# First modulation of layer 0 taken in two halves of rows, with the first weight slot of the projection between them

## The chip, the cores and the metric

The kernel runs on one core of a Trainium2 chip. The metric is the device time in microseconds (us) of one execution; the median of the runs is given. Engines: PE is TensorE (PEld its weight loads), DVE is VectorE, ACT is ScalarE, SP is SyncE, which here only issues transfers.

## The reference, cut to what matters

Two transformer blocks in a row on 256 tokens of width 1024; the change touches only the start of layer 0 of the first block:

```python
c_act = jax.nn.silu(c)                              # (1, 1024)
mod = c_act @ ada_w[layer] + ada_b[layer]           # 6 x 1024 columns
sh1, sc1, g1, sh2, sc2, g2 = split(mod, 6)
h = _rms_norm(x, norm_mix[layer]) * (1.0 + sc1) + sh1
proj = h @ w_in[layer]                              # 1952 columns, first of the mixer
```

So the first projection needs the shift `sh1` (columns 0 to 1023 of `ada_w`) and the scale `sc1` (columns 1024 to 2047). Feature k of `h`, and with it row k of `w_in`, needs only element k of each.

## The kernel before, in words

All weights come as one stream of slots in the order of `plan()`, each at most 128 x 2048 floats (1 MB), into a ring of four slots (`RING`). SP issues the loads in that order (`Sync.load_to`, L398); before load m it waits until the last user of load m - 4 is done (`last_use`). A projection weight is split by ACT into a high part (`whi`, L384) and by DVE into the rest (`wlo`, L338), half a slot at a time (a "chunk"), and PE multiplies each block of 128 rows three times (high by high, low by high, high by low, `mm3`, L240) for two halves of the tokens.

The start (functions `pe_start`, `act_start`, `dve_start`). The 2048 modulation columns are made in four units u of 512 columns; each unit takes two slots, rows 0 to 511 and rows 512 to 1023. For a unit,

- `pe_mods` (PE) multiplies the first slot by the vector `cact` into one row of PSUM: eight passes of 512 columns, since there are four blocks of rows at two passes each;
- `dve_mods` (DVE) multiplies and sums the second slot into `modsum` (tile name `gate`) with four instructions, then copies PE's row to `modrow`;
- `pe_mods_turn` (PE) turns both into a column, with 16 matmuls of one column;
- `dve_mods_turn` (DVE) adds the bias and stores four columns of `K.mod`.

Unit 0 and 1 are the shift, 2 and 3 the scale. `pe_mods(u)` waits until `modrow` of u - 1 has left its bank; `pe_mods_turn(u)` waits for `modrow` of u and until `mods` of u - 1 has left the other bank. In between PE transposes x (`pe_turn`, line L249) and spreads the row norms (`pe_along`, to `cbm` by ACT). Then `dve_mod_scale` makes the scale (`sc`), and `dve_mod_t` (DVE) and `act_mod_t` (ACT) make the eight blocks of `h` transposed: DVE multiplies into `aux`, ACT adds the shift (`hT`), DVE makes the rest (`hTl`). The splits of the weight chunks are placed between the blocks by `split_between`: chunk 1 behind block 2, chunk 2 behind block 4, chunk 3 behind block 6. `pe_rows` for key `inA0` (416 columns, two slots, four chunks of two blocks) then multiplies, block k waiting for `hT` and `hTl` of k (`ready`). Behind it come `inD0` and the other projections, whose splits and sums run in an order fixed on each engine.

The SP order at the start is: columns, loads 0 and 1, a constant, loads 2 and 3, x, loads 4 to 10, the other constants (1 MB), loads 11 and on. Loads 0 to 7 are the modulation, 8 and 9 `inA0`, 10 the first slot of `inD0`.

Of the kernel before, what the change touches and what calls it, by code (L numbers as in the profile page):

```python
# [76 lines left out]
def ada(layer, c0, c1):  # L77
    return panels(f"ada{layer}", "ada_w", (layer,), KT, c0, c1)
# [5 lines left out]


def plan():
    p = ada(0, 0, 2048)
    for l in range(2):
        into = [panels(f"inA{l}", "w_in", (l,), KT, 768, 1184), panels(f"inD{l}", "w_in", (l,), KT, 0, 512),
                panels(f"qup{l}", "w_q_up", (l,), 2, 0, 768) + panels(f"kvup{l}", "w_kv_up", (l,), 1, 0, 1024),  # L90
                panels(f"inB{l}", "w_in", (l,), KT, 1184, 1696),
                narrow(f"inV{l}", "w_in", (l,), 512, 768) + narrow(f"inV{l}", "w_in", (l,), 1696, 1952)]
        mod = summed(0, 2048) if l == 0 else []
        behind = {(1, 0), (1, 1), (2, 3), (3, 0)}
        for n, stage in enumerate(into):
            for at, slot in enumerate(stage):
                p.append(slot)
                if mod and (n, at) in behind:
                    p.append(mod.pop(0))
        if l == 0:  # L100
            p += summed(0, 3072) + summed(0, 4096)
        p += tapered(f"out{l}", "w_out", (l,))
        if l == 0:
            ffn = gate_up("ffn", "ffn_w_gate", "ffn_w_up", (0,)) + down("ffnd", "ffn_w_down", (0,))
            mod = summed(0, 5120) + [slot for c in range(0, 6144, 1024) for slot in summed(1, c)]
            for n, slot in enumerate(ffn):
                p += [slot] + (mod[n - 2:n - 1] if n > 1 else [])
        else:
            for e in range(NE):
                p += gate_up(f"moe{e}", "moe_w_gate", "moe_w_up", (0, e))  # L110
                p += down(f"moe{e}d", "moe_w_down", (0, e))
    w = "w_in_2"
    xbc = blocks_t("xbc", w, (0,), list(range(XBC0, XBC0 + 4096, 128)))
    p += xbc[:5] + panels("dt", w, (0,), KT, DT0, DT0 + 32) + xbc[5:]
    for c in (Q0, K0, V0):
        p += narrow("qkv0", w, (0,), c, c + 512)
    p += panels("z", w, (0,), KT, Z0, Z0 + 2048)
    p += panels("gs", w, (0,), KT, GS0, GS0 + 1024)
    p += panels("sproj", "w_ssd_proj_2", (0,), 16, 0, D)
    for g in (1, 2):  # L120
        for c in (Q0, K0, V0):
            p += narrow(f"qkv{g}", w, (0,), c + 512 * g, c + 512 * g + 512)
    p += narrow("ga", w, (0,), GA0, GA0 + 1024)
    p += panels("aproj", "w_attn_proj_2", (0,), 4, 0, D)
    p += tapered("out2", "w_out_2", (0,))
    p += blocks_t("up2", "w_up_2", (0,), [c for b in range(FT) for c in (128 * b, FF + 128 * b)])
    p += down("down2", "w_down_2", (0,))
    return p
# [400 lines left out]
def pe_start(K, pe):  # L529

    pe_mods(K, pe, 0)
    pe_mods(K, pe, 1)
    pe_mods_turn(K, pe, 0)
    pe_mods(K, pe, 2)
    pe_mods_turn(K, pe, 1)
    pe_turn(K, pe, "nm0", lambda j, i: K.x[:, i, 128 * j:128 * j + 128], KT, "v")
    pe_mods(K, pe, 3)
    pe_mods_turn(K, pe, 2)
    pe_along(K, pe, "nm0")
    pe_mods_turn(K, pe, 3)  # L540


# [14 lines left out]
def dve_start(K, v):  # L557
    v.wait_ge(K.s_cols, 32)
    v.wait_ge(K.act, "rout_hi")
    v.tt(K.rout[:, 1, :], K.col("router", 0, 64), K.rout[:, 0, :].bitcast(F32), ALU.subtract, key="rout_lo")  # L560
    ang, n, r = K.ang, K.angn, K.angr
    v.copy(K.posf[:, :], K.posi[:, :])
    for i in range(2):
        v.ts(ang[:, i, :], K.col("invf", 0, 16), K.posf[:, i:i + 1], None, ALU.mult)
    for t, (shift, quarter) in enumerate(((0.0, 0.0), (0.25, float(np.float32(np.pi / 2))))):
        v.ts(n[:, :, :], ang[:, :, :], float(np.float32(1 / (2 * np.pi))), shift, ALU.mult, ALU.add)
        v.ts(n[:, :, :], n[:, :, :], MAGIC, None, ALU.add)
        v.ts(n[:, :, :], n[:, :, :], MAGIC, None, ALU.subtract)
        if t:
            v.wait_ge(K.act, ("turn", 0))  # L570
        v.stt(r[:, :, :], n[:, :, :], -TWO_PI_1, ang[:, :, :], ALU.mult, ALU.add)
        v.stt(r[:, :, :], n[:, :, :], -TWO_PI_2, r[:, :, :], ALU.mult, ALU.add)
        v.stt(r[:, :, :], n[:, :, :], -TWO_PI_3, r[:, :, :], ALU.mult, ALU.add)
        v.ts(r[:, :, :], r[:, :, :], quarter, 3.1415925, ALU.add, ALU.min)
        v.ts(r[:, :, :], r[:, :, :], -3.1415925, None, ALU.max, key=("angle", t))
    K.dve.here("angles")
    dve_mods(K, v, 0)
    dve_mods(K, v, 1)
    dve_mods_turn(K, v, 0)
    dve_eps(K, v, "nm0")  # L580
    dve_root(K, v, "nm0")
    dve_mods(K, v, 2)
    dve_mods_turn(K, v, 1)
    dve_mods(K, v, 3)
    dve_mods_turn(K, v, 2)
    v.split_to(1)
    dve_mods_turn(K, v, 3)


def act_squares(K, a, s, p, c0, c1, after):  # L590
# [22 lines left out]
def dve_eps(K, v, s):  # L613
    v.wait_ge(K.act, (s, "sq", 0, 1))
    v.ts(K.ssq[:, 0:2], K.ssq[:, 0:2], EPS, None, ALU.add, key=(s, "eps"))
# [120 lines left out]
            a.act(K.hT[:, j, :], K.rtmp4[:, j % 4, :], ACT.Identity, bias=shift[:, j:j + 1], key=(s, "hi", j), own=False)  # L736


def dve_mod_scale(K, v, layer, which, gain):
    v.stt(K.sc[:, :], K.mod[:, layer, 8 * which + 8:8 * which + 16], 1.0, K.col(gain, 0, 8), ALU.add, ALU.mult)  # L740
    v.last()


# [1 line left out]
    return K.mod[:, layer, 8 * which:8 * which + 8]  # L745


def dve_mod_t(K, v, s, scale, shift=None):

    def low(j):  # L750
        v.wait_ge(K.act, (s, "hi", j))
        src, hi = K.rtmp4[:, j % 4, :], K.hT[:, j, :].bitcast(F32)
        if shift is None:
            v.tt(K.hTl[:, j, :], src, hi, ALU.subtract, key=(s, "lo", j), own=False)
        else:
            v.stt(K.hTl[:, j, :], src, shift[:, j:j + 1], hi, ALU.add, ALU.subtract, key=(s, "lo", j), own=False)
    v.wait_ge(K.act, (s, "along"))
    for j in range(KT):
        v.wait_ge(K.pe, (s, "t", j // 2 * 2))
        if j >= 4:  # L760
            v.wait_ge(K.dve, (s, "lo", j - 4))
        v.stt(K.rtmp4[:, j % 4, :], turned(K, j, TURNED.get(s, (4, 5, 6, 7))), scale[:, j:j + 1], K.along, ALU.mult, ALU.mult,
              key=(s, "v", j), own=False)
        if j:
            low(j - 1)
        split_between(K, v, s, j)
    low(KT - 1)


def pe_rows(K, pe, key, lhs, kt, banks=(0, 1, 2, 3), by=(("dve", 0), ("dve", 1)), block=None, at_part=None):  # L770
# [85 lines left out]
def pe_mods(K, pe, u):  # L856

    pe.wait_ge(K.act, "cact")
    pe.take(ROW)
    m = K.mods[2 * u]
    pe.wait_ge(K.full[m % RING], 16 * (m // RING + 1))
    for k in range(4):
        pe.mm(K.ps[ROW][0:1, :], K.cact[:, k:k + 1], K.ring[:, m % RING, 512 * k:512 * k + 512], k == 0, k == 3,
              done=("mod", u) if k == 3 else None)
    pe.given(ROW, (K.dve, ("modrow", u)))
# [28 lines left out]


def dve_mods_turn(K, v, u):
    v.wait_ge(K.pe, ("modturn", u))  # L900
    v.tt(K.mod[:, 0, 4 * u:4 * u + 4], K.ps[COLUMN][:, 0:4], K.col("ab0", 4 * u, 4), ALU.add, key=("mods", u))


def pe_broadcast(K, pe, s, banks):
# [322 lines left out]
def pe_mixer(K, pe, l):  # L1227
# [9 lines left out]

    def values(x):
        pe_values(K, pe, s, x, js[x])
    pe_rows(K, pe, f"inA{l}", hrows(K), KT, by=COPIES, block=ready(K, pe, f"nm{l}"))  # L1240
    pe_rows(K, pe, f"inD{l}", hrows(K), KT, by=COPIES, banks=BANKS_D)
    pe.wait_ge(K.s_rest, 32)
    pe.wait_ge(K.dve, (s, "low", "rows"))
# [1447 lines left out]
def vector_program(K, v):  # L2691
    dve_start(K, v)
    for l in range(2):
        if l:
            dve_root(K, v, f"nm{l}")
        else:
            dve_mod_scale(K, v, 0, 0, "nm0")
        dve_mod_t(K, v, f"nm{l}", K.sc, shift_of(K, l, 0))
        if l:
            barrier(K, v, ("ffn", 0))  # L2700
        else:
            v.wait_ge(K.s_rest, 32)
        dve_mixer(K, v, l)
        dve_root(K, v, f"nf{l}")
        dve_mod_t(K, v, f"nf{l}", K.sc, shift_of(K, l, 3))
        barrier(K, v, ("mixed", l))
        if l == 0:
            dve_dense(K, v)
        else:
            dve_moe(K, v)  # L2710
    dve_eps(K, v, "n1")
    v.split_to(K.parts["xbc"][0] + 1)
    dve_root(K, v, "n1")
    v.split_to(K.parts["xbc"][0] + 2)
    dve_mod_t(K, v, "n1", K.col("n1", 0, 8))
    barrier(K, v, ("ffn", 1))
    dve_ssd(K, v)
    barrier(K, v, "ssd")
    dve_gated(K, v)
    barrier(K, v, "gated")  # L2720
    dve_windows(K, v)
    dve_merge(K, v)
    dve_root(K, v, "n2")
    dve_mod_t(K, v, "n2", K.col("n2", 0, 8))
    barrier(K, v, "second")
    dve_second_ffn(K, v)
    K.dve.here("end")
# [327 lines left out]
```

## Time and profile before

| | us |
|---|---|
| median of 3 runs | 2193.22 |
| the three runs | 2196.7, 2193.22, 2183.3 |
| the profiled execution | 2187.65 |
| span of its trace | 2185.9 |
| PE busy (share of the span) | 2008.5 (92%) |
| DVE busy | 1670.3 (76%) |
| ACT busy | 1329.2 (61%) |

The span runs from the first to the last instruction of the core; the 1.75 us beside it are outside. The stage that the change touches ends 57.9 us after the span's start. The rest of the kernel is the same in both. The clock granted to PE has two levels, 2.4 GHz (shown as 1.00) and 1.2 GHz (0.50).

### The profile page before, as it was taken

The page shows a single profiled execution, that of the slowest core. Times are in us where ns is not written, and L with a number is a line of the kernel's source. Part 1 is how long each engine was busy: PE and PEld are TensorE (multiplying, and loading weights), DVE is VectorE, ACT ScalarE, POOL GpSimd, SP SyncE. Part 2 cuts the span into 40 slices and gives each one's busy share as a digit, 9 for nine tenths or more (in the row PEclk, how much of TensorE's full clock was granted, in tenths as well). Part 3 has the DMA queues.
Part 4 walks back from the last instruction along what each step waited for, and adds up shares of the span by engine and source line. Part 5 has one row for each costly group of instructions (what it writes and reads, how often), then busy time and mean ns, then how long its engine had stood idle before and what let it go on. Part 6 is the DMA issues. An engine that isn't in the chain of part 4 may idle for free. (4 is left out here: it accounts for less than half of the span.)

```text
span 2185.9 us, 28021 instructions
## 1 busy us (share of the span) xinstructions
PE 2008.5 (92%) x11093; PEld 1729.2 (79%) x11093; DVE 1670.3 (76%) x2154; ACT 1329.2 (61%) x1968; POOL 0.2 (0%) x4
## 2 busy tenths in 40 slices
PE   7868999987799999999999999979999988889999
PEld 4668778876788888888888887769877878878987
DVE  5876888676669989998998999768655655567873
ACT  2645443366568777787877777656556544536652
POOL 0000000000000000000000000000000000000000
PEclk8977999998889999999999999989999989889999
DMA  7634788731239989998998998645314532224543
GB/s 292 225 109 151 259 317 329 261 140 39 97 151 368 360 330 366 366 360 325 361 364 341 357 368 316 248 179 181 136 48 154 195 114 97 97 96 143 186 162 108
DMA packets 70090, 497.20 MB, mean 227 GB/s; under 512 B 8000, under 2 KB 8256, under 8 KB 10688
## 3 DMA queue, kind: packets, MB, share of 16 engines
q1 hardware_dynamic: 69664, 494.28, 61.4%
q8 instruction: 90, 1.47, 0.3%
q10 hardware_dynamic: 288, 1.05, 0.1%
q14 instruction: 48, 0.39, 0.0%
HBM read 494.25 MB, written 1.05 MB: 227 GB/s over the span
## 5 line engine op out<-in xcount | busy, mean ns | idle before, releaser
L338 DVE TENSOR_TENSOR wlo<-ring,whi 128x1024 fp32r<-128x1024 f32 (+1 forms) x845 | 1016.6, 1216 | 288.4 <-ACT whi L384 267.4
L384 ACT ACTIVATE whi<-ring 128x1024 fp32r<-128x1024 f32 (+1 forms) x845 | 886.3, 1054 | 517.8 <-PE ps L236 449.8
L236 PE MATMUL ps<-whi,hT 128*128 128x256 f32 (+2 forms) x944 | 324.5, 344 | 26.7 <-DVE hTl L292 6.4
L236 PE MATMUL ps<-wlo,hT 128*128 128x256 f32 (+2 forms) x944 | 318.7, 338 | 0.0
L236 PE MATMUL ps<-whi,hTl 128*128 128x256 f32 (+2 forms) x944 | 318.1, 337 | 0.0
L236 PE MATMUL ps<-whi,xg 128*128 128x512 f32 (+1 forms) x768 | 290.4, 378 | 5.4 <-DVE wlo L338 5.2
L236 PE MATMUL ps<-whi,xgl 128*128 128x512 f32 (+1 forms) x768 | 286.5, 373 | 0.0
L236 PE MATMUL ps<-wlo,xg 128*128 128x512 f32 (+1 forms) x768 | 286.4, 373 | 0.0
L236 PEld LDWEIGHTS ps<-whi,hT 128*128 128x128 f32 x944 | 186.7, 198 | 50.6 <-issue 6.8
L236 PE MATMUL ps<-whi,hf 128*128 128x512 f32 x528 | 209.4, 397 | 11.0 <-DVE wlo L338 4.7
L236 PE MATMUL ps<-wlo,hf 128*128 128x512 f32 x528 | 207.0, 392 | 0.0
L236 PEld LDWEIGHTS ps<-wlo,hT 128*128 128x128 f32 x944 | 186.8, 198 | 16.7
L236 PEld LDWEIGHTS ps<-whi,hTl 128*128 128x128 f32 x944 | 186.0, 197 | 17.5
L236 PE MATMUL ps<-hT,whi 128*128 128x256 f32 (+1 forms) x616 | 176.2, 286 | 5.9 <-DVE hTl L285 4.0
L236 PE MATMUL ps<-hT,wlo 128*128 128x256 f32 (+1 forms) x616 | 175.8, 285 | 0.0
L236 PE MATMUL ps<-hTl,whi 128*128 128x256 f32 (+1 forms) x616 | 174.9, 284 | 0.0
L236 PEld LDWEIGHTS ps<-whi,xg 128*128 128x128 f32 x768 | 145.3, 189 | 31.2 <-DVE wlo L338 6.3
L236 PEld LDWEIGHTS ps<-whi,xgl 128*128 128x128 f32 x768 | 145.2, 189 | 25.7
L236 PEld LDWEIGHTS ps<-wlo,xg 128*128 128x128 f32 x768 | 145.4, 189 | 24.6
L236 PE MATMUL ps<-whi,hf1l 128*128 128x512 f32 x352 | 137.4, 390 | 0.0
L236 PEld LDWEIGHTS ps<-whi,hf 128*128 128x128 f32 x528 | 99.8, 189 | 32.3 <-DVE wlo L338 5.5
L236 PEld LDWEIGHTS ps<-hT,whi 128*128 128x128 f32 (+1 forms) x616 | 117.4, 191 | 6.9 <-ACT hT L364 4.5
(283 smaller groups left out, 2645.1 us busy)
## 6 DMA issues: line engine op xcount, KB each, us to landing
ring<-in_wstream SPq DMA_DIRECT2D x462, 1024.0 KB, 5.0
ring<-in_wstream SPq DMA_DIRECT2D x4, 832.0 KB, 6.0
ring<-in_wstream SPq DMA_DIRECT2D x6, 256.0 KB, 2.7
cst<-in_cst SPq DMA_DIRECT2D x1, 1028.0 KB, 7.7
x<-in_x SPq DMA_DIRECT2D x1, 1024.0 KB, 13.9
work<-in_bias ACTq DMA_DIRECT2D x2, 512.0 KB, 5.0
ring<-in_wstream SPq DMA_DIRECT2D x2, 512.0 KB, 3.8
out_x<-x SPq DMA_DIRECT2D x1, 1024.0 KB, 4.1
```

The costliest lines, as they stand in the source:

```text
L236: i = self.e.matmul(out, lhsT, rhs, start=start, stop=stop, skip_group_check=True)
L338: i = self.e.tensor_tensor(K.wlo[:, q % NS, 0:cols], src, hi.bitcast(F32), ALU.subtract)
L384: i = self.e.activation(K.whi[:, q % NS, 0:cols], K.ring[:, m % RING, at:at + cols], ACT.Copy)
```

## The change

The plan puts units of the first half of the features first: unit 0 (shift, columns 0 to 511) and unit 1 (now the scale's columns 1024 to 1535). Then comes the first slot of `inA0`, then unit 2 (shift 512 to 1023) and unit 3 (scale 1536 to 2047), then the second slot of `inA0`. So loads 0 to 3 are units 0 and 1, load 4 is the first slot of `inA0`, loads 5 to 8 are units 2 and 3, load 9 the second slot; from 10 on all is as before.

PE does units 0 and 1, both turns, the transposes, `pe_along`, `pe_mods(2)`, and then chunks 0 and 1 of `inA0` (blocks 0 to 3). At chunk 2 it does `pe_second_half`: turn 2, `pe_mods(3)`, turn 3. DVE makes scale and blocks 0 to 3, then the sums of units 2 and 3, then scale and blocks 4 to 7. ACT's program is not edited.

```diff
 def plan():
-    p = ada(0, 0, 2048)
+    p = ada(0, 0, 512) + ada(0, 1024, 1536)
...
                 p.append(slot)
+                if (l, n, at) == (0, 0, 0):
+                    p += ada(0, 512, 1024) + ada(0, 1536, 2048)
...
     pe_mods(K, pe, 1)
     pe_mods_turn(K, pe, 0)
-    pe_mods(K, pe, 2)
     pe_mods_turn(K, pe, 1)
     pe_turn(K, pe, "nm0", lambda j, i: K.x[:, i, 128 * j:128 * j + 128], KT, "v")
+    pe_along(K, pe, "nm0")
+    pe_mods(K, pe, 2)
+
+
+def pe_second_half(K, pe):
+
+    pe_mods_turn(K, pe, 2)
     pe_mods(K, pe, 3)
-    pe_mods_turn(K, pe, 2)
-    pe_along(K, pe, "nm0")
     pe_mods_turn(K, pe, 3)
...
     dve_eps(K, v, "nm0")
+    dve_mods_turn(K, v, 1)
     dve_root(K, v, "nm0")
+    v.split_to(1)
+    dve_mod_scale(K, v, 0, 0, "nm0", 0, 4)
+    dve_mod_t(K, v, "nm0", K.sc, shift_of(K, 0, 0), 0, 4)
     dve_mods(K, v, 2)
-    dve_mods_turn(K, v, 1)
     dve_mods(K, v, 3)
     dve_mods_turn(K, v, 2)
-    v.split_to(1)
     dve_mods_turn(K, v, 3)
+    dve_mod_scale(K, v, 0, 0, "nm0", 4, 8)
+    dve_mod_t(K, v, "nm0", K.sc, shift_of(K, 0, 0), 4, 8)
...
-def dve_mod_t(K, v, s, scale, shift=None):
+def dve_mod_t(K, v, s, scale, shift=None, j0=0, j1=KT):
...
-    for j in range(KT):
+    for j in range(j0, j1):
...
-        if j:
+        if j > j0:
             low(j - 1)
...
 def dve_mods_turn(K, v, u):
+    at = (0, 8, 4, 12)[u]
...
-    pe_rows(K, pe, f"inA{l}", hrows(K), KT, by=COPIES, block=ready(K, pe, f"nm{l}"))
+    pe_rows(K, pe, f"inA{l}", hrows(K), KT, by=COPIES, block=ready(K, pe, f"nm{l}"),
+            at_part=None if l else lambda n: pe_second_half(K, pe) if n == 2 else None)
```

## Rows read from the trace of the kernel before

**Rows 1.** The page: its first line, then part 1 (busy time, share, instructions).

```profile
span 2185.9 us, 28021 instructions
...
PE 2008.5 (92%) x11093; PEld 1729.2 (79%) x11093; DVE 1670.3 (76%) x2154; ACT 1329.2 (61%) x1968; POOL 0.2 (0%) x4
```

**Rows 2.** Timeline: start, duration, engine, operation, count [idle before, releaser]; units and turns.

```profile
8.85 6.03 PE L236 MATMUL ps<-ring,cact 128*1 128x512 f32 x8 [8.85 <-DMA ring<-in_wstream]
...
15.65 3.59 PE L236 MATMUL ps<-ring,cact 128*1 128x512 f32 x8 [0.77 <-DVE modrow L306]
...
19.18 0.38 PE L236 MATMUL ps<-cst,modrow 1*128 1x1 f32 x2
...
21.76 0.16 DVE L285 TENSOR_TENSOR mod<-ps,cols 128x4 f32<-128x4 f32 x1 [1.74 <-PE ps L236]
...
22.71 5.29 PE L236 MATMUL ps<-ring,cact 128*1 128x512 f32 x8 [0.98 <-DMA ring<-in_wstream]
...
25.06 0.48 DVE L277 TENSOR_SCALAR gate<-ring,cact 128x512 f32<-128x512 f32 x1 [0.40 <-DMA ring<-in_wstream]
25.59 2.32 DVE L292 SCALAR_TENSOR_TENSOR gate<-ring,cact,gate 128x512 f32<-128x512 f32 x3
...
28.03 0.68 DVE L306 COPY modrow<-ps 1x512 f32<-1x512 f32 x1
...
30.34 3.19 PE L249 MATMUL ps<-cst,x 128*128 128x128 f32 x16
...
33.46 3.98 PE L236 MATMUL ps<-ring,cact 128*1 128x512 f32 x8
...
39.78 0.69 PE L236 MATMUL ps<-cst,rs 128*128 128x128 f32 x4
...
41.02 0.55 PE L236 MATMUL ps<-cst,modrow 1*128 1x1 f32 x2
...
42.02 0.58 PE L236 MATMUL ps<-cst,modrow 1*128 1x1 f32 x2
...
44.18 0.16 DVE L285 TENSOR_TENSOR mod<-ps,cols 128x4 f32<-128x4 f32 x1 [1.45 <-PE ps L236]
```

**Rows 3.** Timeline, same columns: from the weight split to the end of the first projection.

```profile
40.79 1.67 ACT L384 ACTIVATE whi<-ring 128x832 fp32r<-128x832 f32 x2
...
44.38 0.17 DVE L292 SCALAR_TENSOR_TENSOR sc<-mod,cols 128x8 f32<-128x8 f32 x1
...
46.28 0.69 PE L236 MATMUL ps<-whi,hT 128*128 128x416 f32 x1 [2.13 <-DVE hTl L292]
...
46.83 1.02 DVE L338 TENSOR_TENSOR wlo<-ring,whi 128x832 fp32r<-128x832 f32 x1
...
48.28 0.51 ACT L366 ACTIVATE hT<-aux,mod 128x256 fp32r<-128x256 f32 x1 [1.21 <-DVE aux L292]
...
55.50 2.36 DVE L338 TENSOR_TENSOR wlo<-ring,whi 128x1024 fp32r<-128x1024 f32 x2 [0.62 <-ACT whi L384]
...
57.87 0.52 ACT L364 ACTIVATE work<-ps 128x416 f32<-128x416 f32 x1 [1.53 <-PE ps L236]
```

**Rows 4.** Windows: stretch, length; busy PE, PEld, DVE, ACT, POOL; PEclk, DMA share, GB/s.

```profile
24.00:26.00 2.00, 2.00 (x4) 0.33 (x3) 1.46 (x6) 0.00 (x0) 0.00 (x0) 0.51 1.01 426
...
34.00:36.00 2.00, 2.00 (x6) 0.35 (x5) 0.00 (x0) 0.00 (x0) 0.00 (x0) 0.93 0.07 25
...
42.00:44.00 2.00, 2.00 (x9) 1.94 (x9) 0.73 (x1) 0.46 (x1) 0.00 (x0) 0.50 1.03 428
```

**Rows 5.** Windows of line L236 alone: stretch, length, PE, PEld, PEclk, DMA share, GB/s.

```profile
46.28:51.27 4.99, 4.99 (x15) 4.76 (x16) 0.50 0.89 327
51.27:57.87 6.60, 6.60 (x36) 6.58 (x35) 1.00 0.59 214
```

**Rows 6.** DMA issues in 48 to 52 us, and landing times of L413 in 0 to 80 us.

```profile
ring<-in_wstream SPq DMA_DIRECT2D x1, 1024.0 KB, 4.8
...
DMA to landing us min/median/max: 2.7/7.7/12.8
```

More of the change, by code:

```diff
@@ L736, in act_mod_t, with dve_mod_scale @@
             a.act(K.hT[:, j, :], K.rtmp4[:, j % 4, :], ACT.Identity, bias=shift[:, j:j + 1], key=(s, "hi", j), own=False)
-def dve_mod_scale(K, v, layer, which, gain):
-    v.stt(K.sc[:, :], K.mod[:, layer, 8 * which + 8:8 * which + 16], 1.0, K.col(gain, 0, 8), ALU.add, ALU.mult)
+def dve_mod_scale(K, v, layer, which, gain, j0=0, j1=KT):
+    at = 8 * which + 8
+    v.stt(K.sc[:, j0:j1], K.mod[:, layer, at + j0:at + j1], 1.0, K.col(gain, j0, j1 - j0), ALU.add, ALU.mult)
     v.last()
@@ L763, in dve_mod_t @@
               key=(s, "v", j), own=False)
-        if j:
+        if j > j0:
             low(j - 1)
         split_between(K, v, s, j)
-    low(KT - 1)
+    low(j1 - 1)
 def pe_rows(K, pe, key, lhs, kt, banks=(0, 1, 2, 3), by=(("dve", 0), ("dve", 1)), block=None, at_part=None):
@@ L899, in dve_mods_turn @@
 def dve_mods_turn(K, v, u):
+    at = (0, 8, 4, 12)[u]
     v.wait_ge(K.pe, ("modturn", u))
-    v.tt(K.mod[:, 0, 4 * u:4 * u + 4], K.ps[COLUMN][:, 0:4], K.col("ab0", 4 * u, 4), ALU.add, key=("mods", u))
+    v.tt(K.mod[:, 0, at:at + 4], K.ps[COLUMN][:, 0:4], K.col("ab0", at, 4), ALU.add, key=("mods", u))
 def pe_broadcast(K, pe, s, banks):
@@ L2695, in vector_program @@
             dve_root(K, v, f"nm{l}")
[L2696 to L2699, printed above, removed]
+            dve_mod_t(K, v, f"nm{l}", K.sc, shift_of(K, l, 0))
             barrier(K, v, ("ffn", 0))
```

## The prediction, made before the changed kernel was built or run

> **What bounds the kernel now.** I read the page first: PE is busy 92% of the span, DVE 76% [rows 1]. That says what limits the kernel as a whole, not what the edit is worth: it touches only the first 58 us of 2186. So I went to the timeline of 0 to 58 us, and then to the granted clock in windows of 2 us over the same stretch. Behind that stage nothing is edited, and PE and DVE arrive at its end together: DVE finishes its two weight splits at 55.50 + 2.36 = 57.86, and PE's last product frees ACT at 57.87 [rows 3]. Whatever moves this end moves everything behind it, because the ring holds only four slots and each load is released by the work itself. I therefore take the stage's shift one for one.
>
> In the start, PE works nearly without a pause and sets the pace: units at 8.85, 15.65, 22.71 and 33.46, transposes at 30.34, the fourth turn's result at 44.18 [rows 2]. DVE has its sum of unit 2 done by 25.59 + 2.32 = 27.91, and waits for PE afterwards. The scale is made at 44.38, the first product starts at 46.28, the projection ends at 57.87 [rows 3], so its 48 products take 11.6 us.
>
> The same PE work has two prices, by the granted clock. A unit takes 3.59 us where its passes run fast and 6.03 at the very start; the third and fourth took 5.29 and 3.98, partly at half rate [rows 2]. A turn takes 21.76 - 19.18 = 2.6 us fast; a quarter of it takes 42.02 - 41.02 = 1.0 us at the low clock, so 4.1 the whole [rows 2], and the windows show 0.50 there [rows 4]. Of the projection, 15 matmuls took 4.99 us at 0.50 (0.333 each), and 36 took 6.60 us at 1.00 (0.183 each) [rows 5]. The clock was low after the turns, which are matmuls of one column, and rose only after 5 us of dense products.
>
> **The change part by part.** It removes nothing: the same eight sums, four turns and 48 products run; DVE makes the scale with two instructions of 0.17 us rather than one. It changes what waits for what.
>
> *Start, as before to 21.9.* Units 0 and 1 and turn 0 keep their times. Turn 1 comes next at 21.95; 2.6 us, and a little more since the clock had fallen in the window from 24.00 [rows 4]: 24.9. DVE's bias and root (six small instructions, about 1.1 us) lie beside the transposes, which take 3.19: 28.1. `pe_along` 0.69: 28.8 [rows 2]. ACT then copies it (0.4) and splits chunk 0 (1.67 / 2 = 0.84), DVE splits its rest (1.02) [rows 3], and the scale is made at 31.2. Load 4 is released by `pe_mods(0)` as before, and its landing let PE start at 22.71 [rows 2], so the slot is there 6 us before ACT wants it.
>
> *First four blocks.* From scale to first product is 46.28 - 44.38 = 1.9 us [rows 3]: 33.1. PE must first do `pe_mods(2)` from 28.8: 32.4 fast, 34.8 slow. I take fast: the fourth unit directly behind the transposes had a clock of 0.93 in 34 to 36 us [rows 4]. DVE's part: `hT` of block 3 was ready 48.28 + 0.51 - 44.38 = 4.4 us behind the scale, and the rest takes 0.5 more: DVE is free at 36.2. PE's 24 products end at about 37.8 fast (DVE sets the pace), 33.1 + 24 x 0.333 = 41.1 slow.
>
> *Second half.* Here lies the price. Before, units 2 and 3 were summed on DVE while PE lagged behind. Now the sum of unit 2 stands in DVE's queue behind the four blocks, and PE can't turn without it:
>
> - sum of unit 2 and copy of the row on DVE: 25.59 + 2.32 - 25.06 = 2.85, plus 0.68 [rows 2]: 36.2 to 39.8. PE, done at 37.8, stands for 2 us.
> - turn 2: 2.6 to 4.1. It starts behind a pause and is one-column work, so the clock falls inside it; 3.3: 43.1.
> - `pe_mods(3)`: 3.6 to 6.0. It starts at the low clock; 5.8: 48.9. DVE's sum of unit 3 (2.85, from 39.8) is hidden.
> - copy of the row 0.68, bias of turn 2 0.16 and two releases, since PE's turn 3 waits for both: 49.9.
> - turn 3, again with a fall in it: 3.2: 53.1; bias and scale: scale starts at 53.3.
> - to the first product of block 4: 1.9 as above, and the split of chunk 2, which now comes ahead of its `hTl`: 1.02, less a wait of 0.2 that it fills: 2.75: 56.1.
> - 24 products, all behind sparse work: 15 at the low clock 4.99, 9 at 0.183 1.65 [rows 5]: 6.6: 62.7.
>
> Against 57.87 that is +4.9 us. All of the second half at the high clock gives 39.8 + 2.6 + 0.1 + 3.6 + 0.9 + 2.6 + 0.2 + 2.75 = 52.55, and the last blocks then go by DVE (about 4.9, as two splits of 1.02 lie between them): 57.45, -0.4 us. All at the low clock from 33.1 on: 41.1 + 4.1 + 0.1 + 6.0 + 0.9 + 4.1 + 0.2 + 2.75 + 8.0 = 67.3, +9.4 us. The middle is nearer to what the trace shows: each stretch with turns was followed by 0.50 [rows 4].
>
> *Transfers.* Load 8 (DVE's half of unit 3) now takes the ring place of load 4, and so waits for DVE's split of chunk 1: 46.83 + 1.02 - 44.38 = 3.5 us behind the scale, so 34.7. SP's queue behind it holds loads 9 and 10, the other constants and all later loads. A 1 MB load issued alone landed after 4.8 us [rows 6]: 39.5, just where DVE wants it; it is truly late only if DVE's sum starts after 48.9 - 2.85 = 46.0, that is if it lands over 11.3 us after issue. The longest seen is 12.8 [rows 6], a cost of 1.5 at most. Load 9 is wanted at 54, load 10 at 59; both are issued by 40. Load 11 waits for `pe_mods(3)`, 48.9 rather than 38.8; its data are wanted by DVE past 63. I cost all of these at 0, hidden by DVE's and PE's chain above.
>
> *Behind the stage.* DVE ends its part at about 59.2, splits the two chunks (2.36) by 61.6 and then waits for PE. All that follows is 4.9 us late. Nothing there gives it back: before, both engines met at 57.9 without slack [rows 3].
>
> **The rivals.**
>
> 1. *The clock holds, and the overlap only balances.* The first four blocks keep PE at 2.4 GHz through the pause and the turns: -0.4 us, 2189.8 on the mean of the runs given below. For it: a turn right behind a unit ran fast to its end (2.6 us at 19.18 [rows 2]). Against: behind the last two turns the clock was 0.50 [rows 4], and now there is a pause too. Chance 0.22.
> 2. *The overlap pays.* PE reaches block 4 as soon as it once reached block 0, 46.3 and a split, 1 us: 24 products of 6.6 end at 53.9, -4.0 us, 2186.2. For it: most of the projection's first half is indeed off the path. Against: the chain from 36.2 (sum, turn, unit, turn) would have to take 11 us rather than 20, and DVE's order puts the sum behind the blocks. Chance 0.06.
> 3. *Slow from the start of the blocks.* The transposes leave the clock low: `pe_mods(2)` ends at 34.8 and four blocks at 8.0 end at 42.8, 3.0 behind DVE's row at 39.8. Turn 2 and all behind it are later by that: +7.9, 2198.1; with the later low-clock bounds, up to +11. It decides once the blocks end after 39.8. The row speaks against (0.93 in 34 to 36, behind transposes and one unit's beginning [rows 4]). Chance 0.12.
> 4. *Load 8 is the bound.* The other side of 1%: it must land over 11.3 + (22 - 4.9) = 28 us after its issue, for 2212 and more. With 12.8 the longest [rows 6], chance 0.02 at most.
>
> On rival 3 the Trainium skill has a rule (TensorE: Matmul & The Clock Gate, Part 4: PE-mode transpose): the full rate does not engage for transposes. By it the sum would be the 7.9 above rather than 4.9; the window at 34 us does not agree, though a unit had begun in the meantime.
>
> **How the numbers follow.** Forecast, +2 to +7 us, likeliest +4.9: 0.60; rivals 0.22, 0.06, 0.12 (rival 4 inside the last). The sum is made on the profiled execution, 2187.65 (span 2185.9 and 1.75 around it), giving 2192.5. That execution lies 5.6 under the median of 2193.22, and the four times known spread over 13 us, more than the effect. Their mean is 2190.2, so I say 2195. The range takes the bounds of the sum with most of that spread: from 2184 (2183.3 with rival 1 or a little over) to 2206 (2196.7 + 9.4). About 1% (22 us) is what a measurement of this kernel can tell from no change. No case reaches it but a double accident: slower 0.03, faster 0.01, same 0.96.
>
> **What would show it.** In the trace after: first product near 33 and not 46; PE idle near 38 to 40, released by the row copy of DVE; `pe_mods(3)` nearer 6 than 3.6 us; block 4's first product near 56 and the copy out of the projection near 62.7; granted clock 0.50 in most of 41 to 61. A turn 2 that starts before 39, or a clock of 1.00 through the second half, would prove the forecast wrong and rival 1 or 2 right; blocks 0 to 3 ending past 40 would show rival 3. If the projection ends at 62.7 and the whole is not about 5 us later, the step "one for one" is wrong.

## The result: 0.36% slower, within the band of no change

| | kernel before | changed kernel |
|---|---|---|
| median of 14 runs, us | 2189.28 | 2196.02 |
| lowest and highest | 2181.53, 2196.7 | 2191.12, 2199.95 |
| ratio, 95% interval | | 1.0036, 1.0022 to 1.0049 |
| span of the (first) trace | 2185.9 | 2188.4 |
| copy out of the first projection starts | 57.87 | 61.73 |

The interval is 5 to 11 us. It excludes zero, and lies far below the 1% of the forecast's outer classes. The changed kernel's times also spread less (9 against 15 us); no run shows why. Two slow executions of the kernel before, of 3298 and 6804 us, taken beside the first experiments, are left out of all figures.

The start of the changed kernel, from its timeline (start, duration, engine, line, operation, count, and in brackets the idle time before and who ended it; the lines of the code are two further on than before). Each row answers one of [rows 2] or [rows 3]:

```profile
21.68 0.38 PE L238 MATMUL ps<-cst,modrow 1*128 1x1 f32 x2 [0.25 <-DVE mod L287]
...
25.21 3.65 PE L251 MATMUL ps<-cst,x 128*128 128x128 f32 x16
...
29.49 3.59 PE L238 MATMUL ps<-ring,cact 128*1 128x512 f32 x8
...
31.74 0.15 DVE L294 SCALAR_TENSOR_TENSOR sc<-mod,cols 128x4 f32<-128x4 f32 x1
...
33.62 0.43 PE L238 MATMUL ps<-whi,hT 128*128 128x416 f32 x1 [0.54 <-DVE hTl L294]
...
36.77 0.49 DVE L279 TENSOR_SCALAR gate<-ring,cact 128x512 f32<-128x512 f32 x1
...
39.53 0.67 DVE L308 COPY modrow<-ps 1x512 f32<-1x512 f32 x1
...
40.26 0.38 PE L238 MATMUL ps<-cst,modrow 1*128 1x1 f32 x2 [1.63 <-DVE modrow L308]
...
48.06 0.68 DVE L308 COPY modrow<-ps 1x512 f32<-1x512 f32 x1 [4.91 <-PE ps L238]
...
49.00 0.38 PE L238 MATMUL ps<-cst,modrow 1*128 1x1 f32 x2 [0.97 <-DVE mod L287]
...
51.78 0.16 DVE L294 SCALAR_TENSOR_TENSOR sc<-mod,cols 128x4 f32<-128x4 f32 x1
...
54.33 0.69 PE L238 MATMUL ps<-whi,hT 128*128 128x416 f32 x1 [2.78 <-ACT hT L368]
...
61.73 0.52 ACT L366 ACTIVATE work<-ps 128x416 f32<-128x416 f32 x1 [2.63 <-PE ps L238]
```

The first product comes 12.7 us earlier than in the first trace of the kernel before, and it does not help: PE then stands idle three times, for DVE's row copy (40.26), for the next row copy and bias (49.00) and for the first block of the second half (54.33). The kernel before had PE idle for about 2 us only once behind the transposes, ahead of its first product [rows 3]. The granted clock, from windows of the same trace (the last three columns are PEclk, DMA share, GB/s):

```profile
24.00:28.00 4.00, 4.00 (x19) 3.97 (x20) 0.97 (x6) 0.00 (x0) 0.00 (x0) 0.50 0.68 283
...
44.00:48.00 4.00, 4.00 (x7) 0.55 (x5) 0.00 (x0) 0.23 (x1) 0.00 (x0) 0.71 0.79 318
48.00:52.00 4.00, 2.58 (x17) 2.36 (x16) 1.19 (x5) 0.00 (x0) 0.00 (x0) 1.00 0.74 251
...
56.00:60.00 4.00, 4.00 (x13) 3.81 (x12) 3.20 (x6) 2.49 (x3) 0.00 (x0) 0.50 0.67 233
```

### The profile page after: what moved, and what is told of

It reads as the page before. It is cut to its first block and busy times, and to the rows that moved or that the text cites. A ratio compares the mean times of both kernels' runs of the same rounds, so it can differ in the third digit from the quotient of the medians.

```text
span 2188.4 us, 28019 instructions
## 1 busy us (share of the span) xinstructions
PE 2008.4 (92%) x11093; PEld 1728.9 (79%) x11093; DVE 1671.1 (76%) x2155; ACT 1328.8 (61%) x1968; POOL 0.2 (0%) x4
## 3 DMA queue, kind: packets, MB, share of 16 engines
q10 hardware_dynamic: 288, 1.05, 0.1%
HBM read 494.25 MB, written 1.05 MB: 226 GB/s over the span
```

## The experiments

Two questions stood after the result. Is the chain that the forecast summed (DVE's sum behind the blocks, then turn, unit, turn at a varying clock) what sets the end of the stage, or is it the loads? And why is the whole 6.7 us slower when the stage in this pair of traces is only 3.9 later and the span 2.5 longer? All traces at a glance; "stage end" is the start of the copy out of the first projection, and S1 and S2 are the starts of the scale of the first and the second half (`sc`):

| kernel | S1 | turn 2 starts | S2 | stage end | S1 to stage end | span | ratio to before, 95% |
|---|---|---|---|---|---|---|---|
| before, first trace | | | | 57.87 | | 2185.9 | |
| before_again | | | | 53.49 | | 2182.3 | |
| before_third | | | | 55.10 | | 2189.3 | |
| before_fourth | | | | 53.49 | | 2182.0 | |
| changed, first trace | 31.74 | 40.26 | 51.78 | 61.73 | 29.99 | 2188.4 | 1.0036 (1.0022 to 1.0049) |
| after_again | 30.69 | 39.20 | 50.63 | 60.38 | 29.69 | 2193.1 | |
| e1_sum2_early | 31.13 | 37.95 | 49.37 | 59.08 | 27.95 | 2188.8 | 1.0021 (0.9999 to 1.0043) |
| e2_fill | 30.32 | 38.82 | 50.25 | 58.76 | 28.44 | 2189.1 | 1.0045 (1.0024 to 1.0067) |
| e3_sum_splits_early | 29.99 | 36.81 | 48.18 | 56.83 | 26.84 | 2185.5 | 1.0019 (0.9999 to 1.0040) |
| e4_stream_only | | | | 60.52 | | 2192.2 | 1.0039 (1.0015 to 1.0062) |
| e5_sum2_twice | 32.92 | 44.32 | 57.81 | 67.81 | 34.89 | 2187.7 | |
| e6_splits_and_fill | 31.42 | 38.2 | 49.55 | 57.85 | 26.43 | 2185.0 | 1.0018 (0.9995 to 1.0041) |
| e7_before_splits_fill | | | | 52.14 | | 2185.8 | 0.9971 (0.9954 to 0.9988) |
| e8_turns_apart | 29.83 | 36.7 | 48.69 | 56.77 | 26.94 | 2185.2 | 1.0004 (0.9988 to 1.0021) |

Each stage figure of e1 to e8 rests on one trace. Up to S1 the changed kernel, after_again, e2 and e5 run the same program, and S1 still scatters from 30.32 to 32.92; so the column "S1 to stage end" compares the experiments on the second half better than the stage end does.

### The kernel before, three more times

> The kernel before once more, for the scatter of its own trace. Theory (what differs between traces of one kernel is where the granted clock falls): the end of the first projection within 1.5 us of 57.9, and the rest of the trace shifted against the first one by steps of 1 to 5 us at few places (135 to 142, 300 to 570, 1900 to 1960 us). Rival (the changed kernel harms a later stage by itself): no such steps between two traces of the kernel before.

> A third trace of the kernel before. Its projection ended at 57.87 in the first trace and at 53.49 in the second, where the load for unit 2 landed at 21.6 rather than 22.7 and the granted clock stayed at 1.00 until 37. Theory (the start of the kernel before has two forms by that clock): 53 to 54.5, with unit 2 begun before 22 and a clock of 1.00 from 20 to 36, or 57 to 58.5 with a fall at 24. Rival (the first trace was a stray): all further ones at 53.5.

> A fourth trace, with the same two expectations: 53 to 54.5 or 57 to 58.5 by the clock between 24 and 28, against a further value near 53.5 under the rival.

The stage of the kernel before ended at 57.87, 53.49, 55.10 and 53.49. So the first expectation, within 1.5 us of 57.9, failed. The first trace, on which the forecast was made, had the latest end of the four. Timeline of before_again:

```profile
21.64 3.59 PE L236 MATMUL ps<-ring,cact 128*1 128x512 f32 x8 [0.22 <-DVE mod L285]
...
27.57 1.94 PE L249 MATMUL ps<-cst,x 128*128 128x128 f32 x16
...
29.45 3.59 PE L236 MATMUL ps<-ring,cact 128*1 128x512 f32 x8
...
39.70 0.17 DVE L292 SCALAR_TENSOR_TENSOR sc<-mod,cols 128x8 f32<-128x8 f32 x1
...
53.49 0.52 ACT L364 ACTIVATE work<-ps 128x416 f32<-128x416 f32 x1 [1.82 <-PE ps L236]
```

Windows of 24 to 28 us, first before_again, then before_third:

```profile
24.00:28.00 4.00, 4.00 (x23) 2.82 (x22) 3.68 (x8) 0.00 (x0) 0.00 (x0) 1.00 0.99 395
```

```profile
24.00:28.00 4.00, 4.00 (x21) 2.72 (x19) 3.61 (x7) 0.00 (x0) 0.00 (x0) 0.92 1.04 419
```

In before_again unit 2 followed turn 0 at once, released by DVE's bias, and ran in 3.59 us; the clock stayed at 1.00 to about 37, so the transposes took 1.94 us. In the first trace PE waited until 22.71 for the load of unit 2, the clock fell at 24, and the unit took 5.29 and the transposes 3.19 us [rows 2, 4]. I had offered two forms, 53 to 54.5 and 57 to 58.5; the fourth trace fits the first, but the third lies between them (unit 2 at 21.74 but transposes of 3.36 us at a fallen clock), so it is a spread and not a pair.

The second expectation, that the rest of a trace differs by steps, held. From 54 to 128 us DVE's instructions in before_again and before_fourth agree within 0.1 us. The windows around that point read, before_again first:

```profile
124.00:128.00 4.00, 3.06 (x16) 1.83 (x14) 3.36 (x6) 2.31 (x10) 0.00 (x0) 0.50 0.00 0
128.00:132.00 4.00, 3.97 (x18) 3.97 (x19) 3.05 (x4) 0.00 (x0) 0.00 (x0) 0.50 0.00 0
```

```profile
124.00:128.00 4.00, 2.57 (x17) 1.51 (x13) 3.39 (x6) 2.27 (x10) 0.00 (x0) 0.76 0.00 0
128.00:132.00 4.00, 4.00 (x24) 4.00 (x25) 2.93 (x4) 0.00 (x0) 0.00 (x0) 0.67 0.00 0
```

By 140 us before_again is 3.9 us behind, by 320 us 6.6. It made this up again by the end (spans 2182.3 and 2182.0), but the third trace, 1.6 us behind at the end of the stage and 0.7 at 128 us, ended at 2189.3. So what happens behind the stage in one execution moves the end by as much as the whole effect studied here. The step at 128 to 140 us goes with the granted clock, as the windows show; for the later steps the clock was not traced as closely. A single pair of spans can't size it; the stage itself can be read.

### The changed kernel once more

> The changed kernel once more, for the scatter of its start. Theory (DVE's chain and the clock set the stage): turn 2 starts at 40.3 again within 0.3 us, since DVE's row copy sets it; the end of the projection lies between 57.5 and 64 us, by where the granted clock falls (61.73 in the first trace). Rival (the 3.9 us of the stage are chance): it could end at 58 or lower.

The stage ended at 60.38, inside the 57.5 to 64; turn 2 started at 39.20, not within 0.3 us of 40.3, because DVE's blocks began 1.05 us earlier. From S1 to turn 2 it took 8.51 us here and 8.52 in the first trace. DVE's row copy still released PE:

```profile
39.20 0.38 PE L238 MATMUL ps<-cst,modrow 1*128 1x1 f32 x2 [1.63 <-DVE modrow L308]
```

Mean stage end: before (57.87 + 53.49 + 55.10 + 53.49) / 4 = 55.0, changed (61.73 + 60.38) / 2 = 61.1. The difference, 6.1 us, agrees with the 6.7 us of the medians, as far as four traces and two can say.

### The sum ahead of the blocks

```diff
 def dve_start(K, v):
...
     dve_root(K, v, "nm0")
+    dve_mods(K, v, 2, row=False)        # the sum alone
     v.split_to(1)
     dve_mod_scale(K, v, 0, 0, "nm0", 0, 4)
     dve_mod_t(K, v, "nm0", K.sc, shift_of(K, 0, 0), 0, 4)
-    dve_mods(K, v, 2)
+    dve_row(K, v, 2)                    # the copy of PE's row
     dve_mods(K, v, 3)
```

> DVE sums unit 2 before the first weight split, where it idled 4.1 us, and only the row copy stays behind the four blocks. Theory (the sum behind the blocks delays turn 2): turn 2 starts when PE has ended block 3, about 38.7 rather than 40.3, PE's pause of 1.6 us is gone, and the projection ends 1.5 to 4 us earlier than in the changed kernel, near 59. Rival A (load 8 or 9 is the bound): no change of the end, 61.7, since load 8 is still released by the split of chunk 1. Rival B (only the clock counts): the start of turn 2 moves, but the end does not by more than its scatter.

Turn 2 started at 37.95, directly behind the last product of block 3, without a pause; the stage ended at 59.08. Against the two traces of the changed kernel that is 2.65 and 1.3 us earlier. Counted from S1, which takes out the scatter of the start, turn 2 came 1.7 us earlier and the stage end 2.0 and 1.7 us, at the low end of the 1.5 to 4 expected. DVE then waited 2.88 us for load 8 before the sum of unit 3, which cost nothing, since PE's unit 3 took until 45.6. Rival B (only the start of turn 2 moves) fails by this one trace only weakly; e3 and e5 carry more.

### The sum twice

```diff
     dve_mod_t(K, v, "nm0", K.sc, shift_of(K, 0, 0), 0, 4)
+    dve_mods(K, v, 2, row=False, named=False)
     dve_mods(K, v, 2)
```

> The sum of unit 2 on DVE is made twice behind the four blocks, which adds 2.85 us at that place alone. Theory (this place of DVE is on the path): turn 2 starts at 43.1 rather than 40.3 and the projection ends 2.8 us later, 64.5, give or take 2 for the clock. Rival A (loads bound the second half): end stays 61.7.

The sum is made a second time with the same values. Turn 2 and the end:

```profile
44.32 0.58 PE L238 MATMUL ps<-cst,modrow 1*128 1x1 f32 x2 [4.51 <-DVE modrow L308]
```

```profile
67.81 0.52 ACT L366 ACTIVATE work<-ps 128x416 f32<-128x416 f32 x1 [2.69 <-PE ps L238]
```

The 4.51 us pause is the 1.63 of the changed kernel plus 2.88: the place is on the path of turn 2, one for one. From turn 2 to the end it took 23.5 us rather than 21.5 and 21.2; the turn itself now ran at half rate (0.58 us rather than 0.38 a pair) and took 4.1 us rather than 2.5. So the end moved by 6.1 and 7.4 us, to 67.81, beyond the 62.5 to 66.5 foreseen; 1.2 and 2.2 us of it came from a later start of the blocks. Counted from S1 the end moved by 4.9 and 5.2 us: here the longer pause cost its length, and 2.0 to 2.3 us more at the low clock.

### Splits in DVE's idle time too

```diff
 # against e1_sum2_early
     dve_row(K, v, 2)
-    dve_mods(K, v, 3)
+    dve_mods(K, v, 3, row=False)
+    v.split_to(4)                       # chunks 2 and 3; ACT's splits likewise ahead of block 4
     dve_mods_turn(K, v, 2)
+    dve_row(K, v, 3)
```

> As e1 (sum of unit 2 in DVE's idle time), and the splits of chunks 2 and 3 are made while DVE waits for PE's unit 3, and the bias of turn 2 ahead of the row copy. Theory: block 4's first product comes 1.2 us earlier than e1's 51.9, near 50.7, the last blocks no longer wait for splits, and the projection ends near 57.5 (57.87 before): the whole loss of the change is gone, but hardly any gain is left, +-0 on the kernel. Rival (loads bound it): load 9, which came at 43.3 in the changed kernel, holds up the splits and the row copy of unit 3, and turn 3 starts later than 46.6.

```profile
39.29 3.59 PE L238 MATMUL ps<-ring,cact 128*1 128x512 f32 x8
...
42.54 1.96 DVE L340 TENSOR_TENSOR wlo<-ring,whi 128x832 fp32r<-128x832 f32 x2 [1.34 <-ACT whi L386]
...
45.30 0.35 PE L238 MATMUL ps<-cst,modrow 1*128 1x1 f32 x2 [2.42 <-DVE modrow L308]
...
50.07 0.68 PE L238 MATMUL ps<-whi,hT 128*128 128x416 f32 x1 [2.13 <-DVE hTl L294]
...
56.83 0.52 ACT L366 ACTIVATE work<-ps 128x416 f32<-128x416 f32 x1 [3.20 <-PE ps L238]
```

From the scale to the first product of block 4 it took 1.89 us rather than 2.55, and the stage ended at 56.83, 0.7 before the expected 57.5 (from S1, 1.1 us sooner than e1). With the clock up, PE had unit 3 done in 3.59 us, at 42.9, and now the splits did hold up the row copy, by 1.6 us: DVE's two splits, themselves waiting for load 9 (ACT waited 7.2 us for it), ended at 44.5. So the rival is partly right in this kernel: once DVE's chain is shortened, load 9, released behind load 8, is next. On the whole the ratio was 1.0019, not clearly different from 1; but 56.83 is still 1.8 us behind the mean of the kernel before, so "the whole loss of the change is gone" was reckoned against a trace that was no fair base.

### Filling PE's pauses

```diff
 def pe_second_half(K, pe):
+    pe_fill(K, pe, 7)                   # hT by hT, 512 columns, into bank 5
     pe_mods_turn(K, pe, 2)
     pe_mods(K, pe, 3)
     pe_mods_turn(K, pe, 3)
+    pe_fill(K, pe, 11)
```

> The changed kernel with extra products into an unused PSUM bank where PE stood still: 7 of 512 columns ahead of turn 2 and 11 behind turn 3. The result is not used. Theory with the clock as the main term: pe_mods(3) and the last 24 products run mostly at 2.4 GHz; the projection ends near 58 to 59, 3 us earlier than 61.7, though the fill can itself delay the first product of block 4 by up to 0.5 us. Rival (the turns bring the clock down whatever stands beside them): the clock is 0.50 in 43 to 46 and 54 to 60 as in the changed kernel, end 61.7 or a little more.

> As e3, with 10 products of 512 columns into an unused bank behind turn 3, result unused. Theory (chain and clock are the only two terms): block 4 at 50.7 to 51.2, last 24 products in about 5 us rather than 7 as with the fill of e2, end near 56, 2 us before the kernel before; on the whole kernel -1 to -3 us. Rival (the fill only delays): end as e3 or later.

The products of the fill are extra work and are read by nobody. In e2, in the stretch with block 4 and what follows it:

```profile
52.00:56.00 4.00, 4.00 (x16) 3.60 (x15) 3.63 (x8) 2.62 (x5) 0.00 (x0) 0.68 0.49 143
56.00:60.00 4.00, 4.00 (x22) 3.73 (x21) 3.28 (x5) 2.81 (x4) 0.00 (x0) 1.00 0.86 350
```

The stage ended at 58.76, within the 58 to 59 expected. The last 24 products took 58.76 - 53.66 = 5.1 us rather than 7.4 and 7.2, at 1.00 where the changed kernel had 0.50 in 56 to 60. But the fill itself held up block 4, which started 3.4 us behind the scale rather than 2.55; from S2 to the stage end the gain is 1.2 to 1.4 us (8.51 against 9.95 and 9.75). The fill before turn 2 did nothing for unit 3 (4.93 us, against 5.29 and 5.00). In e6:

```profile
49.18 3.53 PE L238 MATMUL ps<-hT 128*128 128x512 f32 x10
...
49.55 0.16 DVE L294 SCALAR_TENSOR_TENSOR sc<-mod,cols 128x4 f32<-128x4 f32 x1
...
57.85 0.52 ACT L366 ACTIVATE work<-ps 128x416 f32<-128x416 f32 x1 [2.84 <-PE ps L238]
```

Block 4 started 2.96 us behind the scale rather than e3's 1.89, and the last 24 products took 5.3 us rather than 6.8. So from S2 the fill gave 0.35 us (8.30 against 8.65). The end, 57.85, is nevertheless 1 us later than e3's and misses the 56 expected, because S2 came 1.4 us later in this trace: S1 was 1.4 us later, before any fill. So the clock term is real, about 2 us in the last products of e2, but the extra products that raised the clock took 0.9 to 1.1 us back, and the whole kernel showed no gain: 1.0045 and 1.0018.

### The stream's order alone

```diff
 # kernel before, with the plan of the changed one
     dve_mods_turn(K, v, 1)
+    v.split_to(2)                       # chunks 0 and 1, so that load 8 is released
     dve_mods(K, v, 3)
     dve_mods_turn(K, v, 2)
-    v.split_to(1)
     dve_mods_turn(K, v, 3)
...
 # ACT: a.split_to(2) ahead of act_root
```

> Only the order of the stream is changed (units paired by half, the first weight slot of the projection between them); PE and DVE keep the order of the kernel before, and chunks 0 and 1 are split early so that load 8 is released. Theory (the order on DVE and PE costs, not the stream): the slot in between delays the load for pe_mods(2) by 2.3 us (25.0 rather than 22.7), so the projection ends 0 to 2.3 us after 57.9. Rival (the stream's order is what costs): end 61 or later, as in the changed kernel, with DVE or PE waiting for load 7 or 8.

```profile
23.50 5.08 PE L238 MATMUL ps<-ring,cact 128*1 128x512 f32 x8 [2.05 <-DMA ring<-in_wstream]
...
38.95 0.49 DVE L279 TENSOR_SCALAR gate<-ring,cact 128x512 f32<-128x512 f32 x1 [5.83 <-DMA ring<-in_wstream]
...
42.72 0.58 PE L238 MATMUL ps<-cst,modrow 1*128 1x1 f32 x2 [3.30 <-DVE mod L287]
...
60.52 0.52 ACT L366 ACTIVATE work<-ps 128x416 f32<-128x416 f32 x1 [2.34 <-PE ps L238]
```

Expected 57.9 to 60.2, measured 60.52: 5.5 us behind the mean of the kernel before, and with the wait for load 8 that the rival named. Here the loads do bind. Unit 2 waits 2.05 us for its load and then takes 5.08 us. The slot in between makes load 8 wait for the split of chunk 1 (33.1), DVE waits 5.83 us for it, and PE's turn 3 comes 3.30 us late at half rate. The stream's order is not free by itself. In the changed kernel this wait is hidden (DVE's sum of unit 3 began at 40.31 without a wait for data, and the row it feeds wasn't wanted before 48), because PE's second half comes late anyway. The ratio here, 1.0039, is like the changed kernel's.

### Turns apart, and the kernel before made better

```diff
 # against e3_sum_splits_early
     pe_mods_turn(K, pe, 0)
-    pe_mods_turn(K, pe, 1)
     pe_turn(K, pe, "nm0", lambda j, i: K.x[:, i, 128 * j:128 * j + 128], KT, "v")
+    pe_mods_turn(K, pe, 1)
...
 # DVE: dve_root ahead of dve_mods_turn(K, v, 1)
```

> As e3, but PE's transposes stand between turn 0 and turn 1, so that no two turns of one-column matmuls follow one another. Theory (two turns in a row bring the clock down in the changed kernel): the granted clock stays 1.00 from 20 to 30, the transposes take 1.9 rather than 3.6 us, and unit 2 starts near 27 (29.5 in the changed kernel); the first product comes near 32, bound by DVE's sum ahead of the split, and the projection ends near 56 (56.83 in e3). Rival (the clock falls at 22 to 24 whatever stands there): transposes 3.2 to 3.7 us and unit 2 at 28.5 or later.

The transposes took 1.94 us as foreseen, and unit 2 began at 26.30, 1.4 us before e3's. But the clock fell all the same within 24 to 28; unit 2 took 5.28 us, and the end, 56.77, is e3's:

```profile
24.00:28.00 4.00, 4.00 (x19) 2.35 (x20) 2.43 (x7) 1.59 (x3) 0.00 (x0) 0.79 0.70 293
28.00:32.00 4.00, 3.88 (x9) 0.82 (x8) 3.75 (x9) 1.28 (x4) 0.00 (x0) 0.78 0.01 2
```

The clock "1.00 from 20 to 30" was wrong, and so was the reason given for the fall, two turns in a row, at least as the whole of it. What stands ahead of the fall is turn 0, transposes and turn 1, without a unit's passes of 512 columns among them; the kernel before has a unit there. The ratio, 1.0004, is the best of the changed kernel's variants, and shows no gain.

```diff
 # kernel before
-    dve_mods(K, v, 3)
+    dve_mods(K, v, 3, row=False)
+    v.split_to(2)
+    dve_row(K, v, 3)
     dve_mods_turn(K, v, 2)
-    v.split_to(1)
+    v.split_to(4)
     dve_mods_turn(K, v, 3)
...
 # ACT: a.split_to(4) ahead of act_root; PE, behind turn 3:
+    for _ in range(2):
+        pe.mm(K.ps[ROW][:, 0:256], K.cst("ident"), K.x[:, 0, 0:256], True, True)
```

> The kernel before, with the splits of chunks 0 to 3 made while DVE and ACT wait for PE's unit 3 and turns, and two extra matmuls of 256 columns (result unused) behind turn 4, so that PE isn't idle before the first product. Theory (the end of the stage is PE's products at the clock they are granted, with DVE's splits between them): the 48 products take 9 to 10 us rather than 11.6 to 11.9; the projection ends 1.5 to 3 us before that of the kernel before with the same start. Rival: products still start at half rate for 5 us and the end moves by under 0.5.

```profile
32.85 1.96 DVE L338 TENSOR_TENSOR wlo<-ring,whi 128x832 fp32r<-128x832 f32 x2 [0.86 <-ACT whi L384]
...
35.82 1.95 DVE L338 TENSOR_TENSOR wlo<-ring,whi 128x832 fp32r<-128x832 f32 x2
...
39.29 2.05 PE L236 MATMUL ps<-x,cst 128*128 128x256 f32 x4
...
39.66 0.17 DVE L292 SCALAR_TENSOR_TENSOR sc<-mod,cols 128x8 f32<-128x8 f32 x1
```

The stage ended at 52.14, 1.35 us before the two traces of the kernel before with the same start, just short of the 1.5 to 3 foreseen. From scale to end it took 12.5 us rather than 13.8. The 48 products took 10.6 us, not 9 to 10. The whole kernel is 0.9971 of the kernel before (0.9954 to 0.9988), the one version whose interval lies on the faster side. That interval is 2.6 to 10 us. Against the mean of four traces the stage is 2.9 us earlier, which lies inside it; its middle, 6.4 us, is more, and whether anything beyond the stage adds to it stays open.

## Why the prediction was right, point by point

The steps against the first trace of the changed kernel:

| step | forecast | measured |
|---|---|---|
| transposes end, `pe_along` ends | 28.1, 28.8 | 28.9, 29.6 |
| scale of the first half | 31.2 | 31.74 |
| first product | 33.1 | 33.62 |
| DVE free for the sum of unit 2 | 36.2 | 36.7 |
| PE's pause ahead of turn 2 | 2 us | 1.63 |
| turn 2 starts | 39.8 | 40.26 |
| turn 2 | 3.3 | 2.5 |
| `pe_mods(3)` | 5.8 | 5.3 |
| turn 3 | 3.2 | 2.6 |
| scale to block 4's first product | 2.75 | 2.55 |
| last 24 products to the copy | 6.6 | 7.4 |
| stage end | 62.7 | 61.73 |
| shift against the first trace of the kernel before | +4.9 (62.7 - 57.87 is 4.8) | +3.9 |
| shift against the mean of four traces | | +6.1 |
| whole kernel, medians | 2195 (+4.9) | 2196.02 (+6.7) |

**The chain.** Right: PE waits for DVE's row at 40.26, as foreseen, and e5 shows that this place is on the path of turn 2 one for one. The sum's position behind the blocks is worth 1.7 to 2.0 us of the loss (e1, counted from S1), the split between scale and block 4 another 0.7 (e3). No run takes away the rest of the chain (turn, unit, turn), so its share of the loss is argued and not shown.

**The clock.** Right in part, and each of the sizes off by under 1 us. I had the clock fall inside both turns of the second half (3.3 and 3.2 us); both ran at 1.00 to their end (2.5, 2.6) and the clock fell behind them. The unit between them ran mostly at the low level, and the last products took 7.4, not 6.6. Errors of both signs cancelled. The sign "0.50 in most of 41 to 61" was not met: that stretch has a mean of 0.74, about half of it at 0.50. The step "at the low clock for 15 products" is the term that I sized too small: 16 ran at about 0.35 us apart before the rise at 60.0.

**The base of the comparison.** This is the step that failed. "Against 57.87" took one execution's stage as the kernel's. Four traces give 53.5 to 57.9, and the one I had was the highest. The same trace held the hint: PE waited 0.98 us for a load ahead of unit 2, and the clock fell 1.3 us into the unit [rows 2, 4]; I read the 5.29 and 3.19 us as prices of the kernel and not of that execution. Against the mean, the loss is 6.1 us, not 4.9. What I had not priced is this. The old order puts a unit directly behind turn 0. Where that unit's load was there in time (before_again, before_third, before_fourth and e7, with a wait of 0.22 us at most) it took 3.59 us each time; where it waited (0.98 us in the first trace, 2.05 in e4) it took 5.29 and 5.08. The changed kernel and e1, e2, e3, e5 and e6 put two turns in a row there, and all seven traces read 0.50 to 0.57 in 24 to 26. My transposes of "3.19" came out at 3.65, where the old kernel has 1.94 in its better form. What in the new order brings the clock down, and what that costs the stage, is not shown: e8 took the two turns apart, kept the quick transposes, saw the fall at 26.3 and ended where e3 did. That the total still hit was luck by 1 to 2 us: the base (2190.2) was 0.9 us above the 2189.28 measured later, the shift 1.8 us too small, and the two partly cancelled.

**Transfers at no cost.** Right for the changed kernel. Load 8 was there at 40.3 or before, when DVE came to it (in after_again DVE waited 0.24 us for it); DVE's sum of unit 3 wasn't late. e4 shows how near it is: with the old order of work, the same stream costs DVE 5.83 us of waiting.

**Rivals.** Rival 1 (the clock holds, -0.4): no trace of the changed kernel or its variants shows 1.00 through the second half; e3 comes nearest (1.00 up to 46) and still ends 1.8 us behind the mean of the kernel before. Rival 2 (gain): turn 2 began at 39.2 and 40.3, not before 39. Rival 3 (slow from the blocks on): the clock did stay low through the transposes, but rose at about 29.3 (0.68 in the window of 28 to 30), just ahead of unit 2, which took 3.59 us; the blocks ended at 38.6, before DVE's row. What PE had done from 25.2 to that rise was transposes and `pe_along`; in after_again the clock rose inside the transposes (24.66 to 28.07; 0.58 in 26 to 28, 1.00 in 28 to 30). The Trainium skill says otherwise of such work (TensorE: Matmul & The Clock Gate, Part 4: PE-mode transpose: the full rate does not engage for it); the trace does not agree. Rival 4: nothing near.

**One for one behind the stage.** Not shown by single traces. In the first pair the shift is 3.9 us at 58, 2.0 at 128, 6.4 at 160, about 5.4 from 300 to 1800 and 2.5 at the end; from after_again to the same trace of before it is 2.5, 0.6, 5.0, 5.3 to 10.4 and 7.2. So up to 128 us 1.9 us of the shift were given back, and more was added behind it; such steps appear in pairs of the same kernel too. e5 ended the stage 6.1 us later than the changed kernel's first trace and had the shorter span (2187.7 against 2188.4). What speaks for the step is the sum alone: 6.1 us of stage, 6.7 us of medians.

## What to carry to other kernels

An overlap is worth what the second half's chain allows: here four blocks came off the path, but their DVE work went in front of the sum that PE's next steps needed, and a serial chain of turn, unit, turn was left with nothing beside it. Where an engine idles a few microseconds ahead, put independent work there first: the sum in DVE's 4.1 us before its first split (e1), the splits where DVE waits for PE's unit (e3). The one faster kernel, e7, is the old order with its splits moved into such waits, and two extra matmuls on PE; which of the two gave how much was not separated. And before a shift of a few microseconds is summed against one trace, look at whether that trace's stage holds a wait or a fall of the clock that another execution may not have.

## What was not expected of the hardware

- Two executions of one kernel agreed within 0.1 us on DVE from 54 to 128 us and then parted by 3.9 us by 140 us, where one had a granted clock of 0.50 and the other 0.76 and 0.67. Of a stage of short matmuls and waits, the time is a distribution.
- A load that came 1.1 us later (22.7 rather than 21.6 us or before) stood at the head of a stage that ended 4.4 us later, with a clock that fell behind it; e4, whose load came later still (23.5), shows the same slow unit (5.08 us). In another trace the clock fell at 27.4 without such a wait, and the stage ended 1.6 us later. That the late load is the cause in the first was not tested by itself.
- Behind extra products the clock was up sooner (24 products in 5.1 us in e2 and 5.3 in e6, rather than 7.4 and 6.8), but the products held up the work behind them by 0.9 and 1.1 us, so that the gain was 1.2 to 1.4 us and 0.35.
